# Three sets of seven block products in place of eight in each feed-forward of a two-block transformer kernel, with half of the weight-block sums made by adding transfers

## What is computed

```python
D_MODEL, D_FF, SEQ = 1024, 2816, 256
def swiglu(x, w_gate, w_up, w_down):
    return (jax.nn.silu(x @ w_gate) * (x @ w_up)) @ w_down
# first block, for each layer:
h = h + 0.5 * swiglu(rmsnorm(h, ffn1_norm[l]), ffn1_w_gate[l], ffn1_w_up[l], ffn1_w_down[l])
...                                                  # the mixer (mix1)
h = h + 0.5 * swiglu(rmsnorm(h, ffn2_norm[l]), ffn2_w_gate[l], ffn2_w_up[l], ffn2_w_down[l])
# second block: the same with a norm behind each part as well, mixer mix2, then ple
```

## Time and profile before

| | us |
|---|---|
| median of 3 runs | 2400.19 |
| lowest, highest | 2399.92, 2402.79 |
| span of the profiled execution | 2402.5 |
| TensorE (PE) busy | 2351.7 (98%) |
| VectorE (DVE) busy | 1515.8 (63%) |
| ScalarE (ACT) busy | 1233.8 (51%) |
| GpSimd (POOL) busy | 52.1 (2%) |
| transfers | 399.95 MB, mean 166 GB/s |

### The profile page before, as it was taken

How to read it: one execution, slowest core, us unless ns; L and a number is a source line. 1 busy time by engine, 2 the same in 40 slices (tenths; PEclk the granted TensorE clock), 3 DMA queues, 4 the chain that set the end, 5 groups by cost and what they waited for, 6 DMA issues and landing times.

```text
span 2402.5 us, 31221 instructions
## 1 busy us (share of the span) xinstructions
PE 2351.7 (98%) x12503; PEld 1919.8 (80%) x12503; DVE 1515.8 (63%) x2297; ACT 1233.8 (51%) x2053; POOL 52.1 (2%) x66
## 2 busy tenths in 40 slices
PE   8999999999999999999999999999999999999997
PEld 6788878888788887888878878778877887877886
DVE  5657786655555678765565567775566557776555
ACT  5446555544544655554454454654455446365445
POOL 0000000000000000000000000000000000000000
PEclk9999999999999999999999999999999999999999
DMA  7554445556555544555545653165555554225553
GB/s 252 179 201 149 133 139 184 184 183 194 174 188 181 173 132 133 175 183 194 187 164 192 194 157 98 46 200 185 192 165 175 190 185 146 83 89 183 178 199 118
DMA packets 110737, 399.95 MB, mean 166 GB/s; under 512 B 12288, under 2 KB 12672, under 8 KB 110336
## 3 DMA queue, kind: packets, MB, share of 16 engines
q1 hardware_dynamic: 110592, 397.96, 50.5%
HBM read 396.86 MB, written 1.05 MB: 166 GB/s over the span
## 4 chain that ended last, share of the span: by engine, by line
PE 90%; DVE 6%; ACT 3%; issue 1%; POOL 0%; DMA 0%; SPq 0%; ACTq 0%; DVEq 0%
PE ps L510 80%; PE ps L517 4%; DVE wlo L488 2%; PE ps L2078 1%; PE ps L1484 1%; PE ps L1448 1%; DVE alo L658 1%; ACT whi L481 1%; DVE xs L919 1%; PE ps L1439 0%; PE ps L2484 0%; ACT ahi L639 0%; DVE tm L2048 0%; PE ps L499 0%; PE ps L2602 0%
## 5 line engine op out<-in xcount | busy, mean ns | idle before, releaser
L488 DVE TENSOR_TENSOR wlo<-raw,whi 128x1024 fp32r<-128x1024 f32 (+1 forms) x748 | 892.9, 1211 | 289.5 <-ACT whi L481 284.9
L481 ACT CAST whi<-raw 128x1024 fp32r<-128x1024 f32 (+1 forms) x748 | 764.5, 1040 | 357.7 <-PE ps L510 347.6
L510 PE MATMUL ps<-whi,ahi 128*128 128x512 f32 (+2 forms) x2016 | 798.7, 396 | 18.1 <-DVE wlo L488 13.6
L510 PE MATMUL ps<-wlo,ahi 128*128 128x512 f32 (+2 forms) x2016 | 793.8, 394 | 0.0
L510 PE MATMUL ps<-whi,alo 128*128 128x512 f32 (+2 forms) x2016 | 789.9, 392 | 0.0
L510 PEld LDWEIGHTS ps<-whi,ahi 128*128 128x128 f32 x2016 | 380.0, 189 | 110.3 <-DVE wlo L488 26.9
L510 PEld LDWEIGHTS ps<-whi,alo 128*128 128x128 f32 x2016 | 380.1, 189 | 74.5 <-issue 1.3
L510 PEld LDWEIGHTS ps<-wlo,ahi 128*128 128x128 f32 x2016 | 380.3, 189 | 71.5 <-issue 1.5
L510 PE MATMUL ps<-whi,yhi 128*128 128x512 f32 (+1 forms) x948 | 372.5, 393 | 2.5 <-DVE ylo L840 1.4
L510 PE MATMUL ps<-wlo,yhi 128*128 128x512 f32 (+1 forms) x948 | 370.7, 391 | 0.0
L510 PE MATMUL ps<-whi,ylo 128*128 128x512 f32 (+1 forms) x948 | 369.3, 390 | 0.0
(11 more groups left out here) (375 smaller groups left out, 1504.8 us busy)
## 6 DMA issues: line engine op xcount, KB each, us to landing
raw<-stream SPq DMA_DIRECT2D x718, 512.0 KB, 3.9
raw<-stream SPq DMA_DIRECT2D x16, 388.0 KB, 3.2
bcb<-bcs SPq DMA_DIRECT2D x9, 512.0 KB, 5.1
raw<-stream SPq DMA_DIRECT2D x8, 416.0 KB, 3.6
raw<-stream SPq DMA_DIRECT2D x4, 384.0 KB, 3.0
cst<-consts SPq DMA_DIRECT2D x1, 1260.0 KB, 8.2
msc<-misc SPq DMA_DIRECT2D x1, 1160.0 KB, 6.7
xs<-xin SPq DMA_DIRECT2D x2, 512.0 KB, 4.4
```

Of the source, the lines that this page charges most:

```text
L481: act.do.copy(whi[:, n % NSP, 0:w], raw[:, n % NRAW, 0:w]).then_inc(*rounded(n))
L488: dve.do.tensor_tensor(wlo[:, n % NSP, 0:w], raw[:, n % NRAW, 0:w], whi[:, n % NSP, 0:w].bitcast(F), ALU.subtract).then_inc(*rest(n))
L510: m = pe.do.matmul(o, a, b, start=(first and q == 0), stop=(last and q == n - 1))
```

## The change

In each feed-forward, six of the 11 groups are joined in three pairs. Such a pair (a "quad", here also "set") is the product of a 2 x 2 arrangement of activation blocks (token half by half of the 1024 rows) with a 2 x 2 arrangement of weight blocks (half of the rows by gate or up, 512 x 512 each). It is formed with seven block products in place of eight, the scheme of Strassen and Winograd. It needs sums of blocks on both sides:

- of the activations, once a feed-forward (`dve_fold`, `act_fold`): `af` is high + low, `cf` holds four sums, `chi`/`clo` their pair;
- of the weights, for each set: ten buffers `sq` of 128 x 1024. SP loads ten half blocks (`sp_quads`, L540). GpSimd issues four transfers that add a second block from HBM onto a loaded one (`pool_quads`, L548, `accum_op=ALU.add`). DVE forms four more sums (`dve_quads`, L558 and L563). Each of the 14 halves is then split like any piece (L508, L519), so a set has 14 splits in place of 8;
- of the products: ACT copies three partial sums from PSUM (`part_sum`, L1009), DVE adds the others on (L1082, L1085, L1094), then silu and hidden tile on 512 columns (L1014, L1018, L1090, L1097).

The order of the units is now a string for each feed-forward (`FLOW`, 3 or 4 down pieces held for the tail): `h` is a half unit of the first group, `r` a gate/up piece, `d` a down piece, a digit one of the seven products. `yhi`/`ylo` hold 12 columns of blocks in turn, where before 6. Many numbers of `PLAN` between stages change too; one of them moves the last four `ahi` of the feed-forwards behind mix1.

```diff
@@ -106,6 +106,12 @@
 
 LEAD = 5.0
 
+BEAT = {"sum7": ((-4.8, 9.7), (6.8, -21.9)), "sum5": ((5.3, 2.4), (-17.9, 2.1)), "sum6": ((6.8, 1.6), (-8.4, 3.8)),
+        "sum4": ((15.7, 19.8), (11.1, 5.3)), "load": (24.0, 22.3, 18.6, 47.5, 14.2, 16.5, 23.2, 21.3, 21.4, 15.5),
+        "silu": 0.4, "kept": 1.45, "silu0": 0.1, "silu1": 2.3, "yhi": -0.4, "ylo": 0.8, "hid": 4.1, "join0": -0.4,
+        "join5": 1.7, "hid1": 2.0, "hid0": -2.8, "fold": (3.4, 12.7, -13.4, 15.7, 15.1), "turn0": 6.3, "turn1": 3.6,
+        "turn2": 4.9, "split": 0.5}
+
 MM = 0.227
...
     "mix1>ffn2": {
-        "act_norm": (6.64, 6.64, 22.76, 24.3),
...
-        "dve_norm": (6.3, 15.58, 25.3, 25.4),
...
+        "act_norm": (5.74, 8.94, 23.46, 30),
...
+        "dve_norm": (-5, 14.38, 24.9, 30.9),
...
+            else:
+                s, g, p, kp = x
+                if p in (4, 6):
+                    act.wait_ge(summed, s, g, p, kp)
+                elif p in (5, 7):
+                    act.wait_ge(added[QUAD_SLOT[p] + kp], s, g)
+                else:
+                    act.wait_ge(load_q[QUAD_SLOT[p] + kp], s, g)
+                act.do.copy(whi[:, n % NSP, :], sq[:, QUAD_SLOT[p] + kp, :]).then_inc(*rounded(n))
...
     def dve_weights():
-        for n in range(len(pieces)):
...
+        for n, (kind, *x) in enumerate(now_splits):
+            yield round_beat(n) + BEAT["split"]
...
+            if kind == "raw":
...
+                dve.do.tensor_tensor(wlo[:, n % NSP, :], sq[:, QUAD_SLOT[x[2]] + x[3], :], whi[:, n % NSP, :].bitcast(F),
+                                     ALU.subtract).then_inc(*rest(n))
...
+            b, p = {0: (0, 6), 2: (0, 5), 4: (2, 4), 6: (3, 3), 8: (1, 7)}[at]
...
+            sp.do.dma_start(sq[:, at + kp, :], streamed(now_quads[s, g, "block", 2 * b + kp])).then_inc(
+                *load_q[at + kp](s, g))
...
+    def pool_quads(s, g):
+
+        for j, (at, b, kp) in enumerate(((8, 3, 0), (2, 1, 0), (8, 3, 1), (2, 1, 1))):
+            yield max(quad_taken(s, g, 1, 0) - BEAT["load"][j], x_ready(s, 1, 1) + 0.1 * j) + 3.0
+            gp.wait_ge(load_q[at + kp], s, g)
+            gp.do.dma_start(sq[:, at + kp, :], streamed(now_quads[s, g, "block", 2 * b + kp]),
+                            accum_op=ALU.add).then_inc(*added[at + kp](s, g))
...
+        t = quad_taken(s, g, 1, 0)
+        for kp in range(2):
+            yield max(t + BEAT["sum6"][g > 0][kp], round_beat(now_quads[s, g, 1, kp]) + 0.51)
+            dve.wait_ge(rest, now_quads[s, g, 1, kp])
+            dve.wait_ge(added[8 + kp], s, g)
+            dve.do.tensor_tensor(sq[:, kp, :], sq[:, 8 + kp, :], sq[:, kp, :], ALU.add).then_inc(*summed(s, g, 6, kp))
+        for kp in range(2):
+            yield max(t + BEAT["sum4"][g > 0][kp], round_beat(now_quads[s, g, 2, kp]) + 0.51)
+            dve.wait_ge(rest, now_quads[s, g, 2, kp])
+            dve.wait_ge(summed, s, g, 6, kp)
+            dve.do.tensor_tensor(sq[:, 4 + kp, :], sq[:, 4 + kp, :], sq[:, kp, :], ALU.add).then_inc(*summed(s, g, 4, kp))
...
+    FLOW = {3: "hhhhhhhh rrrr 1d2d6d57d43 rrdrrd 1d2d6d57d43 rrdrrd 1d2d6d57d43 rrrrddd",
...
+        def quad(g, q, p):
+            b, a = QUAD[p]
+            o = ps[:, bank_of(s, g, b), :]
+            if p in (1, 2, 5):
+                wait_banks_of(s, g, b)
+            elif p in (6, 7, 4):
+                pe.wait_ge(kept, s, g, {6: 1, 7: 6, 4: 7}[p])
+            else:
+                pe.wait_ge(joined, s, g, 5)
+            if p in (3, 5, 6, 7):
+                pe.wait_ge(fold, s, "rest")
...
+                n, w = quad_piece(s, q, p, kp)
+                pe.wait_ge(rest, n)
...
+                    lh = at2(act_pair, ALL, a[1] + c, slice(128 * a[0], 128 * a[0] + 128)) if isinstance(a, tuple) else (
+                        chi[:, a, c, :], clo[:, a, c, :])
+                    m = yield from gemm(o, [(lh, at2(w, ALL, k, ALL))], 1.36 * kp + 0.68 * k,
+                                        c == 0 and p in (1, 2, 5), c == 3, True)
+                m.then_inc(*dense(s, "p", g, p, kp))
+                freed(n, MM, dense, s, "p", g, p, kp)
...
-                        (at2(y_pair, ALL, j % 6, slice(128 * i, 128 * i + 128)),
...
+    def act_quad(s, g):
+        x = groups_of(s)[g]
+        for k, p in enumerate((1, 6, 7)):
+            yield step_beat(s, x["end"][p]) + BEAT["kept"]
+            act.wait_ge(dense, s, "p", g, p, 1)
+            if k == 0 and not quad_index(s, g):
+                act.wait_ge(fold, s, "diff", 3)
+            if g and k == 0:
+                act.wait_ge(hidden, s, g - 1, 0 if groups_of(s)[g - 1]["kind"] == "quad" else 1)
+            act.do.copy(part_sum[:, k, :], ps[:, bank_of(s, g, 0), :]).then_inc(*kept(s, g, p))
+            if p == 6:
+                yield step_beat(s, x["end"][p]) + BEAT["silu0"]
+                act.wait_ge(joined, s, g, 0)
+                sil_free(s, g, 0)
+                act.do.activation(silq[:, 0, :], part_sum[:, 0, :], ACT.Silu,
+                                  scale=stat[:, 6:7]).then_inc(*silu(s, g, 0))
+        yield step_beat(s, x["end"][4]) + BEAT["silu1"]
...
+        act.do.activation(silq[:, 1, :], ps[:, bank_of(s, g, 0), :], ACT.Silu,
...
+            act.do.mul(yhi[:, y:y + 2, :], ps[:, 3, :].rearrange("p (k t) -> p k t", k=2),
+                       -1.0 if x["kind"] == "quad" else 1.0).then_inc(*h_hi(s, v))
...
+    def dve_fold(s):
+
+        for i in range(2):
+            yield step_beat(s, BEAT["fold"][i])
+            dve.wait_ge(a_lo, s, i, 7)
+            dve.do.tensor_tensor(af[:, :, 128 * i:128 * i + 128], ahi[:, :, 128 * i:128 * i + 128].bitcast(F),
+                                 alo[:, :, 128 * i:128 * i + 128].bitcast(F), ALU.add).then_inc(*fold(s, "whole", i))
+
+        def a(c, i):
+            return af[:, c:c + 4, 128 * i:128 * i + 128]
+
+        yield step_beat(s, BEAT["fold"][2])
+        dve.wait_ge(fold, s, "whole", 1)
+        dve.do.tensor_tensor(cf[:, 0], a(4, 1), a(0, 1), ALU.subtract).then_inc(*fold(s, "diff", 0))
+        dve.do.tensor_tensor(cf[:, 2], a(0, 0), a(0, 1), ALU.subtract).then_inc(*fold(s, "diff", 2))
+        dve.wait_ge(fold, s, "diff", 0)
+        dve.do.scalar_tensor_tensor(cf[:, 1], cf[:, 0], -1.0, a(0, 0), ALU.mult, ALU.subtract).then_inc(*fold(s, "diff", 1))
+        dve.wait_ge(fold, s, "diff", 1)
+        dve.do.scalar_tensor_tensor(cf[:, 3], cf[:, 1], -1.0, a(4, 0), ALU.mult, ALU.subtract).then_inc(*fold(s, "diff", 3))
+        yield step_beat(s, BEAT["fold"][4])
+        dve.wait_ge(kept, s, "fold")
+        dve.do.tensor_tensor(clo[:, :, :, :], cf[:, :, :, :], chi[:, :, :, :].bitcast(F), ALU.subtract).then_inc(*fold(s, "rest"))
...
+        yield step_beat(s, x["end"][2]) + BEAT["join0"]
+        dve.wait_ge(dense, s, "p", g, 2, 1)
+        dve.wait_ge(kept, s, g, 1)
+        dve.do.tensor_tensor(part_sum[:, 0, :], part_sum[:, 0, :], ps[:, banks[1], :], ALU.add).then_inc(*joined(s, g, 0))
+        yield step_beat(s, x["end"][7]) + BEAT["join5"]
+        dve.wait_ge(kept, s, g, 7)
+        dve.do.tensor_tensor(part_sum[:, 2, :], part_sum[:, 2, :], ps[:, banks[2], :], ALU.add).then_inc(*joined(s, g, 5))
+        yield step_beat(s, x["end"][4]) + BEAT["hid1"]
+        dve.wait_ge(silu, s, g, 1)
+        dve.wait_ge(joined, s, g, 5)
+        hid_free(dve, s, g)
+        dve.do.scalar_tensor_tensor(hidq[:, 1, :], part_sum[:, 2, :], stat[:, 7:8], silq[:, 1, :], ALU.mult,
+                                    ALU.mult).then_inc(*hidden(s, g, 1))
+        yield step_beat(s, x["end"][3]) + BEAT["hid0"]
+        dve.wait_ge(dense, s, "p", g, 3, 1)
+        dve.do.tensor_tensor(part_sum[:, 1, :], part_sum[:, 1, :], ps[:, banks[2], :], ALU.add).then_inc(*joined(s, g, 3))
+        dve.wait_ge(joined, s, g, 3)
+        dve.wait_ge(silu, s, g, 0)
+        dve.do.scalar_tensor_tensor(hidq[:, 0, :], part_sum[:, 1, :], stat[:, 6:7], silq[:, 0, :], ALU.mult,
+                                    ALU.mult).then_inc(*hidden(s, g, 0))
```

More of the change, by code:

```diff
@@ L405, in program @@
     load_w = [signal(f"load_w{i}", 16) for i in range(NRAW)]
+    load_q = [signal(f"load_q{i}", 16) for i in range(10)]
+    added = {i: signal(f"added{i}", 16) for i in (2, 3, 8, 9)}
+    summed, fold, kept, joined = signal("summed"), signal("fold"), signal("kept"), signal("joined")
     load_x = [signal(f"load_x{i}", 16) for i in range(2)]
@@ L509, in gemm @@
                     yield (t + MM * q,)
-                m = pe.do.matmul(o, a, b, start=(first and q == 0), stop=(last and q == n - 1))
+                m = pe.do.matmul(o, a, b, start=(first and q == 0), stop=(last and q == n - 1),
+                                 skip_group_check=shared)
                 q += 1
@@ L607, in one @@
                     k += 1
[L608 removed]
+                    start = org(s) + max(plan[k], 13 if name in ("act_post", "dve_post") and PARTS[s - 1][0].startswith("ffn") else -20) if k < len(plan) and not name.startswith("pool") else beat
                     yield start
@@ L780, in pe_ffn @@
```

(45 more changed lines are left out.)

468 lines of the change are left out of this document (279 added, 189 removed), and 19 rows, old and new, of the table PLAN.

## The result

| kernel | median, us | ratio to before, 95% interval |
|---|---|---|
| before | 2401.49 | |
| changed | 2459.06 (2449.29 to 2465.62) | 1.0217 [1.0173, 1.0262] |

The change made the kernel 2.2% slower, where 2354 us, about 2% faster, had been forecast. The four executions of the changed kernel lie 16 us apart, so a difference to its median is known to some 8 us. The profiled execution, the fastest of the four, has a span of 2448.0 us. First the page of the changed kernel: busy time by engine (beside the earlier trace rows), the DMA queues (q1 is SP's, q0 GpSimd's), and the chain that ended last.

The account below looks back on a forecast made before the run. TensorE was taken as the bound: 2402.5 - 65.4 + 2 + 8 + 6 + 3 = 2356.1 us for the profiled span, which lies 2.3 over the median, so 2354 us was forecast; 8-in-10 range 2334 to 2388.

Parts of the forecast that it names:

- Matmuls, -65.4: TensorE in the sets: 288 fewer matmuls at 0.227 us, all on the path, 65.4 us less.
- Durations: Instruction times assumed for DVE and ACT: weight sum 1.222 us, join 0.69, remainder 2.3, silu 0.69; DVE 86% busy.
- Sets in general, +2: All sets: DVE's splits keep up, least slack 0.3 us at ylo; 0.1 us charged each, +2, ends 0 and 29.
- First sets, +8: First set of each feed-forward: activation sums and remainder make splits late, 1.0 us x 8 stages, ends 0 and 22.
- mix1, +6: Two feed-forwards behind mix1: casts ahead of the last four ahi make TensorE wait 3.0 us for alo, twice, +6.
- Tables, +3: First feed-forward, once: DVE's rotary tables stand before the second set's hidden tiles; +3 us, ends 0 and 6.
- Transfers, 0: DMA in the sets: engines 0.91 used over a 47.6 us cycle, adding transfer 3.1 us, no wait, cost 0.
- Rival (c): 16 DMA engines bound the sets: above 4.2 us per adding transfer, cycle 30.8 + 4c; 2544 us at 6.2; chance 0.11.
- The clock, 0: TensorE's clock: granted at full speed, 2.4 GHz, in the step examined; nothing in the change alters it, no cost charged.

Follow-up runs that it names:

- narrow: Changed kernel with set transfers cut to 128 of 1024 columns, instructions and waits kept (result differs, only time counts); 2366.26 us, ratio 0.9841 to before.
- best: Changed kernel with evenly spaced set loads, old order behind mix1, later rotary tables, second hidden tile ahead of activation sums, product 2's blocks earlier; 2374.04 us, ratio 0.9876.

## Why the prediction was wrong, step by step

**Matmuls, -65.4: right.** 288 fewer, at the same pace: 92 in 20.98 us of the changed kernel's chain, 0.228 us each.

**Durations: right.** Sum of weight blocks 1.221 us (taken 1.222), join 0.68 (0.69), remainder 2.29 (2.3), silu of 128x512 0.70 (0.69), hidden tile 0.75. DVE was busy 1861 us ("near 1900").

**Sets in general, +2: right.** narrow has no wait of TensorE over 0.25 us in any set after a first one, but for the one of the tables.

**First sets, +8: right in size, which is luck, not in place.** In narrow no split of a first set is late; the transposes ahead of it wait for a hidden tile that stands behind the four sums of activations:

```profile
PE ps L592 <- DVE hid L1071: 7.2, 8, 1.9
```

In best, with the tile in front, the wait is where I had put it, at the split behind the remainder, and larger.

**mix1, +6: right in the wait, short in what it cost.** Changed has this row, and its like at 1074.95 (start, length, engine, what [idle before, releaser]); the figure was 3.0:

```profile
457.77 0.78 PE L584 MATMUL ps<-whi,ahi 128*128 128x512 f32 x1 [3.12 <-DVE alo L771]
```

Behind it TensorE ran 3.4 us at a granted clock of 0.50, its lower level of 1.2 GHz, as it did from 1075.6 us:

```profile
457.80:461.20 3.40, 3.40 (x8) 2.72 (x9) 0.69 (x3) 0.00 (x0) 2.78 (x4) 0.50 1.05 380
```

Matmuls began 0.43 us apart there in place of 0.227, 1.7 us more for each of the two waits. The prediction took the clock as full throughout ("nothing below changes that").

**Tables, +3: right.** One wait of 2.35 us for hidq.

**Transfers, 0: the step that failed.** Its price was near (an adding transfer 2.8 us of the engines, taken 3.1), and 0.91 was no underestimate. But it divided demand by the whole cycle of 47.6 us and concluded "no wait, as the first sum that needs an added block comes over 10 us after it is issued, and a load lands in 3.9 us". The 3.9 us of the earlier trace rows belong to a load behind little else. Here eight loads and two adds were issued in the last 25 us before a set (556.66 to 581.68). Measured 2459 - 2366 = 93 us in place of 0. Rival (c) named the right side and resource, and its sign came true (ACT waiting for blocks at a DMA share of 1.04), but by its rule, a cycle of 30.8 + 4c, c of 2.8 lies under its threshold of 4.2 and costs nothing: it failed by the same averaging. I had SP's order at hand and did not follow the loads through the set as I had followed the splits.

**The clock, 0: a smaller step that failed.** It shows in what narrow lies over the sum: its span is 2365.3 us, 9 over 2356.1. That is not more waiting. TensorE's time without work is 68.6 us against 2402.5 - 2351.7 = 50.8 before, 17.8 more, where the sum had charged 2 + 8 + 6 + 3 = 19. That these totals agree is partly luck: at the start of the second block's first stage TensorE waits 1.23, 2.27 and 2.58 us for `xs` and `alo`, where before had 0.31 and 2.11, 3.7 us that I had not looked for. But the mean granted clock is 0.993 in narrow and 0.996 before, by an estimate from these figures 17 against 10 us of full speed lost, part of it while TensorE stood. At that same start it is 0.50 for 10.2 us, and before for 3.4:

```profile
1213.80:1224.00 10.20, 5.89 (x17) 4.58 (x18) 7.50 (x19) 5.93 (x19) 1.15 (x3) 0.50 0.68 225
```

Some 3 us stay open, and so does whether another order of that stage would win its waits: it was not tried.
